# Stick-breaking heads with queries on partitions, reversed scans on VectorE, and four unread products ahead of each recurrence level

## The chip, the core and the metric

One NeuronCore of a Trainium2 chip runs the whole program in one launch. The metric is device time in microseconds (us), the median of several runs. The engines are TensorE (PE in the profile; PEld are its weight loads), VectorE (DVE), ScalarE (ACT), GpSimd (POOL) and SyncE (SP), which issues most DMAs. Each engine runs its own instructions in the order in which they are written, and waits at semaphores.

## What is computed

Two transformer blocks, one after the other, on 512 tokens of width 1024, each with a mixture of experts behind its mixer. The change lies in the mixer of the second block. It has eight stick-breaking heads (width 64) beside four heads of a gated recurrence (width 128); 16 meta tokens stand ahead of the 512. Cut to the stick-breaking heads:

```python
z = einsum('bhtd,bhsd->bhts', q, k) * scale
valid = (s_pos < t_pos) & (s_pos >= LEAD_PAD)
log_keep = where(valid, log_sigmoid(-z), 0.0)
log_tail = lax.cumsum(log_keep, axis=3, reverse=True) - log_keep
w = where(valid, exp(log_sigmoid(z) + log_tail), 0.0)
out = einsum('bhts,bhsd->bhtd', w, v)
```

With softplus(z) = log(1 + exp(-|z|)) + max(z, 0), the exponent of a weight is z minus the sum of the softplus over that key and all later ones. The recurrence is computed in seven levels per head: at each level the products of two decayed factors fill one more part of a 128x128 causal matrix of every 128-token tile.

## The kernel before

The second mixer is 10 turns (`TURNS`) of 4 places (`PLACES`), written out by hand on every engine. Turn i takes up stick-breaking head i, and each place of turns 1 to 7 holds one of the 28 recurrence levels, `step(n)`: GpSimd subtracts decays (`level_diff`), ScalarE exponentiates (`level_exp`), VectorE multiplies (`level_products`, which raises `level_ready`), TensorE takes four 128x128 products (bank L), and VectorE reads them one level later (`level_read`). At level 0 of a recurrence head TensorE also does KT and DG, at level 1 the output HO of the head before, at level 2 the state KV.

A stick-breaking head before: keys lie on partitions, queries along the columns, 1792 columns in five pieces. `scores` gives Z (TensorE), VectorE scales and masks it into `zw`, ScalarE takes Abs and Exp (`stick_exp`) and Ln (`stick_log`), VectorE adds max(z, 0) (`stick_logits`), GpSimd adds up the sums of later key blocks (`sums_of_blocks`), TensorE takes the sums over keys with a triangle of ones (`sums_behind`, bank R), VectorE subtracts them (`stick_subtract`), ScalarE exponentiates (`stick_weights`) and TensorE multiplies with the values (`stick_out`, bank SO). R of head i-1 and SO of head i-2 stand in turn i. Behind turn 7, in turns 8 and 9, come the last heads, the normed rows turned (`mixed_turned`, mT) and split into a high and a low part (`mixed_high` on ScalarE, `mixed_low` on VectorE), and then the output product (`out_product`), which needs mT 4 to 7 for its first half. The loading of the second block's expert weights waits for the last mT, which is issued 24 matmuls into that product. `unread_products(b, count)` issues products of constants whose result nobody reads; before, it is used in the routers and at the head of the expert stage.

```python
def step_after(i, place):
    return PLACES * (i - 1) + place if 1 <= i < SBH else None
```

## Time and profile before

| | us |
|---|---|
| median of 3 runs | 1741.87 (1740.36 to 1744.36) |
| the profiled execution's own time | 1742.63 |
| its span in the profile | 1740.9 |
| PE busy | 1607.4 (92%) |
| DVE busy | 819.9 (47%) |
| ACT busy | 335.7 (19%) |
| POOL busy | 238.3 (14%) |

Times in the profile count from the start of the span. The busy shares are means over stages that differ; the turns of the second mixer are the stretch from about 1029 to 1187 us, 9% of the span, and the rest of the page says little about them.

### The profile page before, as it was taken

What the parts mean: (1) busy time and instruction counts of PE and PEld (TensorE: products, weight loads), DVE (VectorE), ACT (ScalarE), POOL (GpSimd) and SP (SyncE); (2) the same over time, 40 slices, a digit from 0 to 9 for tenths busy, and PEclk for the clock granted to TensorE, in tenths of its full rate; (3) what the DMA queues carried; (4) which work ended last, traced back from release to release, by engine and by line L of the source; (5) the groups of instructions that cost most, each with busy time, mean ns of one, the idle gap of its engine ahead of it and who ended that gap; (6) DMA issues with size and microseconds to landing.
All of it is one profiled execution on the core that took longest, in us unless ns stands there. A gap on an engine that the chain in (4) does not pass through costs nothing.

```text
span 1740.9 us, 19130 instructions
## 1 busy us (share of the span) xinstructions
PE 1607.4 (92%) x7778; PEld 1030.6 (59%) x7778; DVE 819.9 (47%) x1360; ACT 335.7 (19%) x574; POOL 238.3 (14%) x298
## 2 busy tenths in 40 slices
PE   7999999999999896878599988999999998999996
PEld 5688888886888432333488875778643333333332
DVE  7898645536464511111743249985532322332233
ACT  3422000027100210100311154651201010000011
POOL 1100003200000310110200005781120000000000
PEclk9999999999999998999799999999999999999998
DMA  5122222220237999999422200015899999999993
GB/s 203 49 97 97 73 97 97 98 73 25 76 146 284 305 407 409 425 428 414 190 98 73 97 25 1 1 44 220 327 378 430 429 429 429 429 430 430 430 430 143
DMA packets 54080, 403.27 MB, mean 232 GB/s; under 512 B 13776, under 2 KB 15184, under 8 KB 25952
## 3 DMA queue, kind: packets, MB, share of 16 engines
q1 hardware_dynamic: 46560, 389.34, 55.6%
q0 software_dynamic: 7424, 12.61, 2.0%
q8 instruction: 66, 1.08, 0.2%
q14 instruction: 30, 0.25, 0.0%
HBM read 397.69 MB, written 16.81 MB: 238 GB/s over the span
## 4 chain that ended last, share of the span: by engine, by line
PE 72%; DMA 14%; DVE 5%; ACT 2%; issue 2%; POOL 2%; SPq 2%; POOLq 0%; DVEq 0%; ACTq 0%
PE bank L1751 38%; PE bank L738 13%; PE bank L753 6%; DMA arena<-in_expert_in 4%; PE bank L717 2%; DMA arena<-in_expert_gate 2%; DMA ring<-in_expert_up 2%; DMA arena<-in_expert_up 2%; DMA ring<-in_expert_gate 2%; DMA arena<-in_expert_out 2%; DMA ring<-in_expert_in 1%; PE bank L1743 1%; PE bank L718 1%; PE bank L920 1%; PE bank L1862 1%
## 5 line engine op out<-in xcount | busy, mean ns | idle before, releaser
L738 PE MATMUL bank<-arena 128*64 128x512 f32 x960 | 273.8, 613 | 30.1 <-DMA arena<-in_expert_in 12.3
L738 PE MATMUL bank<-ring,arena 128*64 128x512 f32 x576 | 184.1, 618 | 9.9 <-issue 5.4
L738 PEld LDWEIGHTS bank<-arena 128*64 128x64 f32 x960 | 84.0, 140 | 174.9 <-issue 173.9
L1127 DVE TENSOR_TENSOR resid<-resid,bank 128x512 f32<-128x512 f32 x120 | 80.7, 685 | 202.9 <-PE bank L718 202.9
L2435 DVE CAST ring_high<-ring 128x2048 fp32r<-128x2048 f32 x51 | 63.0, 1236 | 238.3 <-DMA ring<-in_stream_a 147.4
L2436 DVE TENSOR_TENSOR ring_low<-ring,ring_high 128x2048 fp32r<-128x2048 f32 x60 | 138.7, 2312 | 6.4 <-ACT ring_high L2107 4.5
L753 PE MATMUL bank<-arena 128*64 128x512 f32 x448 | 114.4, 595 | 14.3 <-DVE arena L1153 7.2
L1751 PE MATMUL bank<-ring_low,xn_high 128*128 128x512 f32 x288 | 113.1, 393 | 0.3 <-DVE ring_low L2436 0.3
L1751 PE MATMUL bank<-ring_high,xn_high 128*128 128x512 f32 x288 | 112.3, 390 | 0.0
L1751 PE MATMUL bank<-ring_high,xn_low 128*128 128x512 f32 x288 | 112.2, 390 | 0.0
L738 PEld LDWEIGHTS bank<-ring,arena 128*64 128x64 f32 x576 | 55.9, 141 | 70.6 <-issue 70.6
L1149 DVE TENSOR_TENSOR arena<-misc,bank 128x256 f32<-128x256 f32 (+1 forms) x32 | 17.6, 551 | 165.5 <-ACT misc L1033 142.5
L1235 POOL DMA_INDIRECT arena<-xn_rows,token_table x32 | 32.6, 1020 | 417.8 <-PE bank L920 382.4
L753 PE MATMUL bank<-ring,arena 128*64 128x512 f32 x288 | 78.6, 596 | 7.1 <-issue 4.5
L753 PEld LDWEIGHTS bank<-arena 128*64 128x64 f32 x448 | 39.4, 137 | 75.9 <-issue 73.0
L1751 PE MATMUL bank<-xn_low,ring_high 128*128 128x512 f32 x192 | 75.8, 395 | 2.3 <-DVE misc L2571 2.3
L1751 PE MATMUL bank<-xn_high,ring_low 128*128 128x512 f32 x192 | 75.5, 393 | 0.0
L1751 PE MATMUL bank<-xn_high,ring_high 128*128 128x512 f32 x192 | 75.4, 393 | 0.0
L1033 ACT ACTIVATE misc<-bank 128x256 f32<-128x256 f32 (+1 forms) x32 | 15.7, 490 | 295.2 <-PE bank L738 295.2
L1267 POOL TENSOR_SCALAR rstd<-ssq 128x1 f32<-128x1 f32 x25 | 11.7, 468 | 422.0 <-ACT arena L1366 259.0
L1119 DVE SCALAR_TENSOR_TENSOR y_low<-bank,gate_slot,y_high 128x512 fp32r<-128x512 f32 x32 | 24.0, 751 | 91.7 <-ACT y_high L1047 91.7
L717 PEld LDWEIGHTS bank<-y_high,spread 128*128 128x128 f32 x128 | 24.0, 187 | 71.7 <-issue 69.0
(395 smaller groups left out, 3067.2 us busy)
## 6 DMA issues: line engine op xcount, KB each, us to landing
ring<-in_stream_a SPq DMA_DIRECT2D x42, 1024.0 KB, 5.1
arena<-in_expert_gate SPq DMA_DIRECT2D x20, 2048.0 KB, 23.7
arena<-in_expert_in SPq DMA_DIRECT2D x18, 2048.0 KB, 27.6
arena<-in_expert_up SPq DMA_DIRECT2D x18, 2048.0 KB, 24.6
arena<-in_expert_down SPq DMA_DIRECT2D x18, 2048.0 KB, 25.1
ring<-in_expert_up SPq DMA_DIRECT2D x12, 2048.0 KB, 25.7
ring<-in_expert_down SPq DMA_DIRECT2D x12, 2048.0 KB, 25.4
ring<-in_expert_gate SPq DMA_DIRECT2D x12, 2048.0 KB, 25.3
```

Source lines behind the costliest of these rows:

```text
L717: nc.tensor.matmul(bank[bank_at][:, :], w, half_of(y_high[:, p % 2, :], half), start=first, stop=False)
L718: ins = nc.tensor.matmul(bank[bank_at][:, :], w, half_of(y_low[p % 2], half), start=False, stop=last)
L738: last = nc.tensor.matmul(h[side * SLOTS:(side + 1) * SLOTS, :], tokens[:, k, side * SLOTS:(side + 1) * SLOTS], w[:, k * 512:(k + 1) * 512 ...
L753: last = nc.tensor.matmul(bank[6 + n][side * SLOTS:(side + 1) * SLOTS, :], hidden[:, f, side * SLOTS:(side + 1) * SLOTS], w[:, f * D + n * ...
L920: last = nc.tensor.transpose(bank[k // 4][:, k % 4 * P:(k % 4 + 1) * P], m.xg[:, p % XG, k * P:(k + 1) * P], c("ident"))
L1119: V.scalar_tensor_tensor(half_of(y_low[p % 2], half), bank[6 + half][:, :], gate_slot[:, p:p + 1], half_of(y_high[:, p % 2, :], half).bitc ...
L1127: nc.vector.tensor_tensor(place, place, bank[bank_at][:, :], ALU.add).then_inc(m.moe_added, 1)
L1149: V.tensor_tensor(m.act[:, 0:m.width], m.sg[:, 0:m.width], up_of(m), ALU.mult).then_inc(m.act_ready, 1)
L1235: G.indirect_dma_start(m.xg[:, p % XG, :], None, m.xn_rows[:, :], bass.IndirectOffsetOnAxis(ap=m.token_table[:, p:p + 1], axis=0), bounds_ ...
L1751: ins = nc.tensor.matmul(b, left(k)[l_], right(k)[r_], start=(first and k == 0 and i == 0), stop=(last and k == KC // 2 - 1 and i == 2))
L2435: then(V.tensor_copy(hi, ring_raw[n % RING]))
L2436: V.tensor_tensor(lo, ring_raw[n % RING], hi.bitcast(F32), ALU.subtract).then_inc(weights_split, 1)
```

## The change

Queries now lie on partitions and keys along the columns, 1344 columns: four 128-column blocks of a query tile against its own keys, masked, and four "rest" pieces of 16, 144, 272 and 400 columns. So the sum over later keys runs along the columns. ScalarE scales the rest pieces from PSUM (`stick_scores`) and VectorE only the four masked blocks; ScalarE writes max(z, 0) as a Relu into `above_zero`; eight VectorE scans over reversed views (`stick_sums`) add both and run the sum, and one 1344-column subtraction gives the exponents. TensorE turns these in 14 transposes (`exponents_turned`, bank WT), ScalarE exponentiates what was turned, from PSUM into `w_turned` (`stick_weights`), and TensorE multiplies as before (`stick_out`). `sums_of_blocks`, `sums_behind`, `stick_logits` and `stick_subtract` are gone. The output of head i-1 now stands in turn i, one turn earlier, and there are 9 turns. Four unread 512-column products stand ahead of each level's wait for `level_ready`. The value projection takes 16 rows of the meta tile instead of 128. The last turned rows come in another order, and two of the last loads of projection weights wait for other units.

```diff
+REST_W = [META + t * P for t in range(NT)]
+REST_AT = [SEQ + sum(REST_W[:t]) for t in range(NT)]
+STICK = SEQ + sum(REST_W)
+SCORE_UNITS = ((), (0, 1, 2), (3,))
+TURNED = 10 * P + SEQ
+TURNED_UNITS = (((0, 0), (0, 1), (0, 2), (0, 3)), ((1, 1), (1, 2), (1, 3), (3, 3)), ((2, 2), (2, 3)))
+TURNED_AT = {at: SEQ * n + P * j for n, unit in enumerate(TURNED_UNITS) for j, at in enumerate(unit)}
...
-        zw = [at(arena, i * STICK, [STICK]) for i in range(3)]
+        zw = [at(arena, i * STICK, [STICK]) for i in (2, 3)]
+        above_zero = at(arena, STICK, [STICK])
+        w_turned = at(ring[1], 0, [TURNED])
...
-                    sp.wait_ge(psum_filled2, U2.filled(("R", SBH - 2, NT2 - 1)))
+                    sp.wait_ge(psum_filled2, U2.filled(("WT", SBH - 2, 3)))
+                if n == first + 2 * len(STREAM2) - 2:
+                    sp.wait_ge(psum_filled2, U2.filled(("SO", SBH - 1)))
...
+                def product(out, t, keys_):
+                    return nc.tensor.matmul(out, sbq[half, h // 2, t * P:(t + 1) * P], keys_, start=True, stop=True)
+                b = begin2(("Z", h, 0))
+                for t in range(NT):
+                    last_ = product(b[:, t * P:(t + 1) * P], t, sbk[half, h // 2, (t + 1) * P:(t + 2) * P])
+                end2(last_)
+                for j in (1, 2):
+                    b = begin2(("Z", h, j))
+                    for t in SCORE_UNITS[j]:
+                        a = REST_AT[t] - REST_AT[SCORE_UNITS[j][0]]
+                        last_ = product(b[:, a:a + REST_W[t]], t, sbk[half, h // 2, PAD:PAD + REST_W[t]])
                     end2(last_)
...
+            def exponents_turned(g, units):
+                pe.wait_ge(exponents_ready, g + 1)
+                e = zw[g % 2]
+                for j in units:
+                    b = begin2(("WT", g, j))
+                    if j < 3:
+                        for n, (s, t) in enumerate(TURNED_UNITS[j]):
+                            a = t * P if s == t else REST_AT[t] + META + s * P
+                            last_ = nc.tensor.transpose(b[:, n * P:(n + 1) * P], e[:, a:a + P], c("ident"))
+                    else:
+                        for t in range(NT):
+                            last_ = nc.tensor.transpose(b[0:META, t * P:(t + 1) * P], e[:, REST_AT[t]:REST_AT[t] + META],
+                                                        c("ident"))
+                    end2(last_)
             def stick_out(g):
-                pe.wait_ge(weight_ready, g + 1)
+                wait_read2(pe, ("WT", g, 3))
                 b = begin2(("SO", g))
                 for t in range(NT):
-                    for s in range(t + 2):
-                        a = STICK_AT[s] + (t - FIRST_T[s]) * P
-                        last_ = nc.tensor.matmul(b[:, t * SBD:(t + 1) * SBD], zw[g % 3][:, a:a + P],
-                                                 sbv[:, s, g * SBD:(g + 1) * SBD], start=(s == 0), stop=(s == t + 1))
+                    out_ = b[:, t * SBD:(t + 1) * SBD]
+                    for s in range(t + 1):
+                        a = TURNED_AT[s, t]
+                        nc.tensor.matmul(out_, w_turned[:, a:a + P], sbv[:, s + 1, g * SBD:(g + 1) * SBD],
+                                         start=(s == 0), stop=False)
+                    last_ = nc.tensor.matmul(out_, w_turned[0:META, META_AT + t * P:META_AT + (t + 1) * P],
+                                             sbv[0:META, 0, g * SBD:(g + 1) * SBD], start=False, stop=True)
                 end2(last_)
             def head_out(g):
...
+                b = begin2(("L", h, lv))
+                unread_products(b, 4)
                 pe.wait_ge(level_ready, n + 1)
-                b = begin2(("L", h, lv))
                 for t in range(NT):
...
                     if place == 0 and i < SBH:
                         scores(i)
-                    if sums_blocks(i, place):
-                        sums_behind(i - 1, sums_blocks(i, place))
-                    if place == 2 and i >= 2:
-                        stick_out(i - 2)
+                    if place == 3 and i >= 1:
+                        stick_out(i - 1)
                     if step_after(i, place) is not None:
                         step(step_after(i, place))
+                    if place in (1, 2) and i >= 1:
+                        exponents_turned(i - 1, (0, 1) if place == 1 else (2, 3))
                     if (i, place) == (SBH, 0):
                         for k in (4, 5):
                             mixed_turned(k)
                         head_out(HGH - 1)
+                        for k in (0, 1):
+                            mixed_turned(k)
                     if (i, place) == (SBH, 2):
-                        mixed_turned(6)
-            for k in TURN_ORDER[3:-1]:
-                mixed_turned(k)
-            out_product(0, (1, 0), lambda part: wait_read2(pe, ("mT", TURN_ORDER[4 * part + 3])),
-                        lambda: mixed_turned(TURN_ORDER[-1]))
+                        for k in (2, 6):
+                            mixed_turned(k)
+            mixed_turned(7)
+            out_product(0, (1, 0), lambda part: wait_read2(pe, ("mT", 3 if part else 7)), lambda: mixed_turned(3))
...
+            def stick_scores(h):
+                if h >= 2:
+                    act.wait_ge(psum_filled2, U2.filled(("WT", h - 2, 3)))
+                for j in (1, 2):
+                    b, ts = unit2(("Z", h, j)), SCORE_UNITS[j]
+                    a, end = REST_AT[ts[0]], REST_AT[ts[-1]] + REST_W[ts[-1]]
+                    read2(A.activation(zw[h % 2][:, a:end], b[:, 0:end - a], ACT.Copy, scale=SBD ** -0.5))
             def stick_exp(h):
                 v = sps[h % 2]
-                act.wait_ge(z_ready, h + 1)
-                A.activation(v, zw[h % 3], ACT.Abs).then_inc(act_step, 1)
+                wait_read2(act, ("Z", h, 0))
+                wait_read2(act, ("Z", h, 2))
+                A.activation(v, zw[h % 2], ACT.Abs).then_inc(act_step, 1)
                 act.wait_ge(act_step, 2 * h + 1)
                 A.activation(v, v, ACT.Exp, scale=-1.0).then_inc(act_step, 1)
             def stick_log(h):
                 v = sps[h % 2]
+                if h >= 1:
+                    act.wait_ge(sums_ready, h)
+                A.activation(above_zero, zw[h % 2], ACT.Relu).then_inc(log_ready, 1)
                 act.wait_ge(act_step, 2 * h + 2)
                 A.activation(v, v, ACT.Ln, bias=1.0).then_inc(log_ready, 1)
             def stick_weights(g):
-                wait_read2(act, ("R", g, NT2 - 1))
-                A.activation(zw[g % 3], zw[g % 3], ACT.Exp).then_inc(weight_ready, 1)
+                for j, unit in enumerate(TURNED_UNITS):
+                    b, w = unit2(("WT", g, j)), P * len(unit)
+                    read2(A.activation(w_turned[:, SEQ * j:SEQ * j + w], b[:, 0:w], ACT.Exp))
+                b = unit2(("WT", g, 3))
+                read2(A.activation(w_turned[0:META, META_AT:META_AT + SEQ], b[0:META, :], ACT.Exp))
...
-            def stick_subtract(g, blocks):
-                for s in blocks:
-                    b = unit2(("R", g, s))
-                    zs = zw[g % 3][:, STICK_AT[s]:STICK_AT[s] + STICK_W[s]]
-                    read2(V.tensor_tensor(zs, zs, b[:, 0:STICK_W[s]], ALU.subtract))
-            def stick_logits(h):
-                dve.wait_ge(log_ready, h + 1)
-                V.scalar_tensor_tensor(sps[h % 2], zw[h % 3], 0.0, sps[h % 2], ALU.max, ALU.add).then_inc(sp_ready, 1)
+                if h >= 2:
+                    dve.wait_ge(psum_filled2, U2.filled(("WT", h - 2, 3)))
+                b = unit2(("Z", h, 0))
+                read2(V.scalar_tensor_tensor(zw[h % 2][:, 0:SEQ].rearrange("p (t s) -> p t s", s=P),
+                                             b[:, :].rearrange("p (t s) -> p t s", s=P), SBD ** -0.5,
+                                             c("strict")[:, None, :].broadcast_to([P, NT, P]), ALU.mult, ALU.add))
+            def sums_from_last(v, a, w, initial):
+                part = v[:, a:a + w][:, ::-1]
+                return V.tensor_tensor_scan(part, part, above_zero[:, a:a + w][:, ::-1], initial, ALU.add, ALU.add)
+            def stick_sums(h):
+                v = sps[h % 2]
+                dve.wait_ge(log_ready, 2 * h + 2)
+                for t in range(NT):
+                    ins = sums_from_last(v, t * P, P, 0.0)
+                then(ins)
+                for t in range(NT):
+                    ins = sums_from_last(v, REST_AT[t], REST_W[t], v[:, t * P:t * P + 1])
+                ins.then_inc(sums_ready, 1)
+                dve.wait_ge(sums_ready, h + 1)
+                V.tensor_tensor(zw[h % 2], zw[h % 2], v, ALU.subtract).then_inc(exponents_ready, 1)
...
-                    if sums_blocks(i, place):
-                        stick_subtract(i - 1, sums_blocks(i, place))
-                    if place == 2 and 1 <= i < SBH or (i, place) == (1, 0):
-                        stick_logits(i if place else 0)
+                    if place == 2 and i < SBH:
+                        stick_sums(i)
+                    if place == 1 and i >= 2:
+                        head_sums(i - 2)
                     if (i, place) == (SBH, 1):
                         last_head_norm()
-                    if place == 1 and i >= 3:
-                        head_sums(i - 3)
+                        mixed_low(0)
+                        mixed_low(1)
                     if (i, place) == (SBH, 2):
+                        mixed_low(2)
                         mixed_low(6)
...
-            def sums_of_blocks(g):
-                v = sps[g % 2]
-                pool.wait_ge(sp_ready, g + 1)
-                for s in range(NT2 - 2, -1, -1):
-                    a, w, behind = STICK_AT[s], STICK_W[s], STICK_W[s + 1]
-                    ins = G.tensor_tensor(v[:, a + w - behind:a + w], v[:, a + w - behind:a + w], v[:, a + w:a + w + behind],
-                                          ALU.add)
-                    if s > 0:
-                        then(ins)
-                ins.then_inc(sums_ready, 1)
...
-                    if place == 3 and 2 <= i < SBH + 1:
+                    if place == 0 and i >= 2:
                         head_square(i - 2)
-                    if place == 2 and i >= 3:
-                        head_norm(i - 3)
-                    if place == 2 and 1 <= i < SBH or (i, place) == (1, 0):
-                        sums_of_blocks(i if place else 0)
+                    if place == 2 and i >= 2:
```

The three places of which the prediction speaks, as the instructions stand on their engines. First ScalarE in turn 5, from the rows of scores on. Before: the exponentials of the weights of head 3 (L2308), Abs and Exp of head 5 (L2297, L2299), the exponentials for recurrence head 3 (L2322 to L2329), a level's exponential (L2318) and Ln (L2304).

```order
L2308 ACTIVATE arena<-arena 128x1792
L2297 ACTIVATE misc<-arena 128x1792
L2299 ACTIVATE misc<-misc 128x1792
L2322 ACTIVATE chunk_decay<-arena 128x5
L2326 ACTIVATE ring<-arena 128x128 x4
L2329 ACTIVATE ring<-arena 128x512
L2318 ACTIVATE resid<-resid 128x512
L2304 ACTIVATE misc<-misc 128x1792
L2318 ACTIVATE resid<-resid 128x512
```

After: two copies of scores (L2320), Abs and Exp (L2326, L2328), the same recurrence exponentials (L2357 to L2364), level (L2353), Relu and Ln (L2334, L2336), level, and the exponentials of the weights of head 4 (L2341, the last of them L2343, not shown).

```order
L2320 ACTIVATE arena<-bank 128x432
L2320 ACTIVATE arena<-bank 128x400
L2326 ACTIVATE misc<-arena 128x1344
L2328 ACTIVATE misc<-misc 128x1344
L2357 ACTIVATE chunk_decay<-arena 128x5
L2361 ACTIVATE ring<-arena 128x128 x4
L2364 ACTIVATE ring<-arena 128x512
L2353 ACTIVATE resid<-resid 128x512
L2334 ACTIVATE arena<-arena 128x1344
L2336 ACTIVATE misc<-misc 128x1344
L2353 ACTIVATE resid<-resid 128x512
L2341 ACTIVATE ring<-bank 128x512 x2
```

The exponentials of the weights moved from ahead of Abs to behind Ln. Second TensorE at the end of turn 5. Before: a level (L2036), the second part of R (L1993, L1996), the next level, and the scores of head 6 (L1985).

```order
L2036 MATMUL bank<-resid 128x128 x4
L1993 MATMUL bank<-ring,cst 128x384
L1996 MATMUL bank<-ring,cst 128x256
L1993 MATMUL bank<-ring,cst 128x256
L1996 MATMUL bank<-ring,cst 128x128
L1993 MATMUL bank<-ring,cst 128x128
L2036 MATMUL bank<-resid 128x128 x4
L1985 MATMUL bank<-arena 128x512 x2
```

After: the last ten products of `stick_out` (L2022, L2024), the unread products (L1301), the level (L2055), and the scores of head 6 (L1987).

```order
L2022 MATMUL bank<-arena,ring 128x64 x3
L2024 MATMUL bank<-arena,ring 128x64
L2022 MATMUL bank<-arena,ring 128x64 x4
L2024 MATMUL bank<-arena,ring 128x64
L1301 MATMUL bank<-count_ones 128x512 x4
L2055 MATMUL bank<-resid 128x128 x4
L1987 MATMUL bank<-arena 128x128 x4
L1987 MATMUL bank<-arena 128x16
```

So `stick_out`, which waits for the exponentials of the weights, now stands ahead of the last level of a turn and of the next scores. Third VectorE in turn 0 and at the start of turn 1. Before: five scans for the decays, the keys (L2719, L2720), the two products that KT and HO need (`head_products`, L2813, L2815), the first level's products (L2769, L2774), and the scores of head 1.

```order
L2726 SCALAR_TENSOR_TENSOR arena<-cst,arena 128x128 x5
L2719 TENSOR_SCALAR arena<-arena,oml 128x528 x4
L2720 MEMSET arena 128x4x112
L2813 TENSOR_TENSOR ring<-ring,arena 128x512
L2815 TENSOR_TENSOR ring<-ring,arena 128x512
L2769 TENSOR_TENSOR resid<-resid,arena 128x4x64
L2774 TENSOR_TENSOR resid<-resid,arena 128x4x64
L2745 TENSOR_SCALAR arena<-bank,cst 128x512
```

After, from the keys' last instruction on: the eight scans and the subtraction of head 0 (L2784, L2796), then `head_products` (L2847, L2849) and the first level.

```order
L2757 MEMSET arena 128x4x112
L2784 SCALAR_TENSOR_TENSOR ring<-ring,arena 128x128 x4
L2784 SCALAR_TENSOR_TENSOR ring<-ring,arena 128x16
L2784 SCALAR_TENSOR_TENSOR ring<-ring,arena 128x144
L2784 SCALAR_TENSOR_TENSOR ring<-ring,arena 128x272
L2784 SCALAR_TENSOR_TENSOR ring<-ring,arena 128x400
L2796 TENSOR_TENSOR arena<-arena,ring 128x1344
L2847 TENSOR_TENSOR ring<-ring,arena 128x512
L2849 TENSOR_TENSOR ring<-ring,arena 128x512
L2803 TENSOR_TENSOR resid<-resid,arena 128x4x64
```

The sums of head 0 stand in front of the first level; they wait for that head's Ln.

## Rows read from the trace of the kernel before

**Rows 1.** The page, part 1: span and TensorE's share.

```profile
span 1740.9 us, 19130 instructions
```

**Rows 2.** Stretches: start, turn 2, turns 3 to 6, turn 7, tail.

```profile
core 0: us, PE busy (x) PEld busy (x) DVE busy (x) ACT busy (x) POOL busy (x), PEclk, DMA share, GB/s
1028.83:1060.36 31.53, 19.70 (x90) 13.88 (x88) 26.82 (x51) 21.40 (x29) 14.32 (x17) 0.78 0.00 1
1060.36:1080.75 20.39, 17.47 (x102) 13.18 (x101) 19.76 (x39) 9.51 (x10) 11.35 (x15) 1.00 0.00 1
1080.75:1154.54 73.79, 72.73 (x450) 57.65 (x449) 68.49 (x130) 41.81 (x53) 57.60 (x71) 1.00 0.00 1
1154.54:1169.80 15.26, 15.26 (x89) 11.68 (x90) 13.88 (x30) 8.42 (x8) 9.55 (x14) 1.00 0.00 1
1169.80:1187.19 17.39, 16.52 (x120) 14.01 (x119) 10.64 (x20) 8.36 (x12) 12.09 (x18) 1.00 0.65 242
```

**Rows 3.** The chain that ended last, turn 7: start, us, what.

```profile
1154.54 3.21 PE bank L1985 x10
...
1158.83 0.86 PE bank L1993 x2
...
1162.06 0.89 PE bank L2036 x8
1162.95 3.07 PE bank L2006 x28
```

**Rows 4.** Instructions in order of time, VectorE: start, us, instruction, idle before.

```profile
1101.18 0.74 DVE L2745 TENSOR_SCALAR arena<-bank,cst 128x512 f32<-128x512 f32 x1
...
1103.42 0.28 DVE L2747 SCALAR_TENSOR_TENSOR arena<-bank,cst 128x128 f32<-128x128 f32 x1
```

**Rows 5.** Groups by line and form in the turns: busy, mean ns, idle before.

```profile
L2758 DVE TENSOR_TENSOR arena<-arena,bank 128x512 f32<-128x512 f32 x16 | 10.6, 681 | 3.7 <-PE bank L1996 3.3 <-DVE resid L2792 0.2 <-DVE ring L2801 0.2
L2762 DVE SCALAR_TENSOR_TENSOR misc<-arena,misc 128x1792 f32<-128x1792 f32 x4 | 8.1, 2022 | 0.3 <-DVE ring L2801 0.2
```

**Rows 6.** In order of time, five scans of 128 columns alone, and beside GpSimd.

```profile
1032.03 1.69 DVE L2726 TENSOR_TENSOR_SCAN arena<-cst,arena 128x128 f32<-128x128 f32 x5
...
1047.05 3.63 DVE L2726 TENSOR_TENSOR_SCAN arena<-cst,arena 128x128 f32<-128x128 f32 x5
...
1044.79 3.87 POOL L2991 TENSOR_TENSOR ring<-ring 128x128 f32<-128x128 f32 x4 [3.41 <-DVE ring L2762]
```

**Rows 7.** A 4-column GpSimd operation beside VectorE's 1792 columns, and all twelve of it.

```profile
1111.89 2.38 DVE L2762 SCALAR_TENSOR_TENSOR ring<-arena,ring 128x1792 f32<-128x1792 f32 x1 [0.15 <-DVE resid L2792]
...
1112.47 1.85 POOL L2970 TENSOR_SCALAR rstd<-rstd 128x4 f32<-128x4 f32 x1
...
L2970 POOL TENSOR_SCALAR rstd<-rstd x12: 192/193/2047, 1094.3 to 1186.6; 128x4 f32<-128x4 f32 x12
```

**Rows 8.** In order of time, ScalarE in the start and in turn 6.

```profile
1036.76 1.26 ACT L2326 ACTIVATE ring<-arena 128x128 f32<-128x128 f32 x4
...
1139.62 0.63 ACT L2318 ACTIVATE resid<-resid 128x512 f32<-128x512 f32 x1 [7.81 <-POOL resid L3008]
...
1143.46 1.70 ACT L2299 ACTIVATE ring<-ring 128x1792 f32<-128x1792 f32 x1
1145.06 0.61 ACT L2318 ACTIVATE resid<-resid 128x512 f32<-128x512 f32 x1
```

**Rows 9.** In order of time, TensorE: unread products in the router.

```profile
1241.81 4.05 PE L1303 MATMUL bank<-count_ones 128*128 128x512 f16 x18
```

**Rows 10.** In order of time, TensorE in the start.

```profile
1038.87 1.12 PE L1911 MATMUL bank<-cst,ring 128*128 128x128 f32 x4 [5.13 <-DVE ring L2813]
...
1048.71 2.07 PE L1993 MATMUL bank<-ring,cst 128*128 128x512 f32 x2 [6.09 <-POOL ring L2991]
...
1052.09 1.02 PE L1993 MATMUL bank<-ring,cst 128*128 128x512 f32 x2
```

**Rows 11.** The chain that ended last, the tail.

```profile
1168.92 0.91 PE bank L2036 x8
...
1181.40 0.45 PE bank L1911 x4
1181.84 3.09 PE bank L2006 x28
...
1186.39 0.75 DVE state_low L2834
1187.19 5.74 PE bank L1751 x24
```

125 lines of the change are left out of this document (47 added, 78 removed).

## The prediction

> **What bounds the kernel now.** The span is 1740.9 us [rows 1]; the execution took 1742.63, the median of the runs is 1741.87. I read first the busy time by stretch [rows 2]: the turns run from 1028.83 to 1187.19. From turn 3 to 6 TensorE is busy 72.73 of 73.79 us and VectorE 68.49, so both are nearly full: 18.4 us a turn. In the start the granted clock is 0.78 of full and TensorE busy 19.7 of 31.5. Then I read the chain that ended last [rows 3, 11]: in turn 7 it stays on TensorE, and the tail is R, SO, the turned rows and one VectorE split ahead of the output product at 1187.19. What comes behind that product moves with it: the expert loads wait for the last mT, 24 matmuls into the product both before and after. So only the product's start counts.
>
> **What a head costs on each engine.** TensorE before: scores 3.21, SO 3.07; the first four of the nine R products (1920 columns) take 1162.06 - 1158.83 = 3.23, all 3072 columns 5.2; a level 0.89 [rows 3]. After: 3.21/1792 x 1344 = 2.4 for scores, 14 transposes at 0.45/4 [rows 11] = 1.6, SO 3.07 again (14 products, the narrow ones no cheaper). That is 11.5 against 7.1. The unread products take (4.05 - 0.38)/17 = 0.216 each [rows 9], the last one's length 0.38 taken off, so 0.86 a level and 3.5 a turn. TensorE gives back 1 us a turn net. Its sum by turn after: 7.1 + 4 x (0.89 + 0.86) + the recurrence's KT, DG, KV, HO (0.45, and 16 more 128-column products at 0.89 per four: 4.0 per seven levels, 2.3 a turn) = 16.4.
>
> VectorE before: scores 1101.18 to 1103.70 = 2.5 [rows 4], max and add 2.0, subtracting 1792 columns in five pieces about 2.5 (0.68 per 512) [rows 5]: 7.0. After: the masked block 0.7; scans: five of 128 columns in 1.69 [rows 6], 0.325 each from start to start; with 0.06 fixed that is 2.07 ns a column, so 1344 columns in eight scans are 2.8 + 0.5 = 3.3; the subtraction 1344/1792 x 2.02 = 1.5 [rows 5]; the link between the two sets of scans 0.15. Sum 5.7, of which 4.95 in one block. Reversed views are not in the trace; I take the forward price, bound it below by the same and above by double (3.3 more a head). GpSimd loses its 3.87 a head [rows 6].
>
> ScalarE: 1792 columns take 1.70, 512 take 0.61 [rows 8], so 0.85 ns a column; 1344 take 1.31. Abs, Exp, Relu, Ln are 5.2, the copies of scores 1.0, the weights' four exponentials 1.95. That is 8.2 against 6.8: ScalarE is far from full, but what matters is where they stand.
>
> **The loop that takes over.** From the order on ScalarE and TensorE: after Ln come a level's exponential (0.54) and the weights (1.95); `stick_out` waits for them (3.07 + 0.1), then unread (0.86), the level (0.89), scores of the next head (2.4 + 0.15 to the last end), last copy 0.5, Abs and Exp 2.65, a level 0.54, Relu and Ln 2.55. Sum 16.2 us a turn, in which no engine is full. The other branch, Ln to sums (4.95) to the level's products (0.67), ends 0.9 us before the unread products do. Into the loop fall, in walking the six turns: turn 2, `head_products` between sums and KT, +1.25; turn 3, the HO copy that ScalarE waits for (+1.1) and 2.0 of recurrence exponentials (1.26 for its four [rows 8], one of 512 and a short one); turn 4, HO on TensorE +1.8; turn 5, again 2.0; turn 6, KT's copy 0.57, KV 0.89 and WT waiting behind HO, +2.7; turn 7 none. Together 97.2 + 10.8 = 108 us. Before, turns 2 to 7 took 1169.80 - 1060.36 = 109.4 [rows 2]. Gain 1.4.
>
> **The start.** In turn 0 the sums of head 0 now stand ahead of `head_products`. ScalarE: copies from 1033.4 to 1034.4, Abs, Exp to 1037.1, recurrence exponentials to 1039.0, level 1039.5, Relu, Ln to 1042.1; sums to 1047.0; KT can start at 1047.7 where it started at 1038.87 [rows 10]. Before, the 9 us were mostly lost again: TensorE idled 6.09 us until 1048.71 for GpSimd's sums and then ran its first product at half speed (1.87 us for 0.86 of work, against the third pair) [rows 10]. After, level 0 ends near 1052.3 (the unread products run at half and then full speed), Ln of head 1 near 1055.9, its sums 1061.1, `stick_out` of head 0 at 1062.1, level 3 at 1063.9. Before, the scores of head 2 began at 1060.36. Loss 3.5.
>
> **The tail.** Before, 17.4 us from the last level to the product [rows 2, 11]: R and two SO (3.07 + 3.09), an exponential between. After: mT 4, 5, HO (waits for the last read; done 3.0 in), the copy and mT 0, 1 to 4.6, WT to 6.1, the weights on ScalarE to 7.4, SO to 10.6, the copy to 11.1; VectorE's squares and row sum to 12.5, then the split of mT 7 to 13.2. Gain 4.1. The load that now waits for the last SO and the re-reading of rows behind it have 11 us and more until they are used; without that cover they would cost about 5.
>
> **The value projection** still streams 512 columns a product: nothing.
>
> **Sharing between VectorE and GpSimd.** Rows 6 and 7 show it: five scans took 3.63 us instead of 1.69 beside GpSimd's sums, and a 4-column operation of GpSimd 1.85 instead of 0.193 beside 1792 columns of VectorE [rows 6, 7]. In the block of sums GpSimd has a level's two subtractions and a head's norm, about 3.1 us. Bounds: nothing, or 3.1 a turn. I take about 1.2; over the 0.9 of slack, and whole in turn 2, that is +1.8 in all.
>
> **Sum.** 3.5 - 1.4 - 4.1 + 1.8 = -0.2, against 1742.63; against the median 1741.7. I say 1741.5.
>
> **Rivals.**
> First, no change to speak of, as summed: 1738.4 to 1745.4, which is within 0.2% (3.5 us, about what a measurement of this kernel tells from no change). Chance 0.38.
> Second, faster: the 10.8 us that I put into the loop run beside it, and TensorE's own 16.4 a turn is the bound. 6 x 16.4 = 98.4 instead of 108, no toll from sharing: 1741.5 - 9.6 - 1.8 = 1730; half of it 1736. For it: GpSimd made ScalarE wait 7.81 us for a level in turn 6 [rows 8], and its sums are gone. Against: ScalarE's order is fixed, and so are `stick_out`'s wait and the three exponentials behind the scores. Chance 0.34.
> Third, slower: the block of sums meets GpSimd's work and is doubled as in rows 6: 3.3 becomes 7.1, less the slack 0.9, +2.9 a turn. Six turns are 17, less the 1.8 already in: 1757; half is 1749. It decides as soon as the block grows by over 0.9. Against: GpSimd has only 3.1 us there, where in that row it worked all the time. Chance 0.20.
> The Trainium skill ("SBUF — State Buffer", Who interferes with whom) says that the pair of ports which VectorE and GpSimd share is an exclusive lock held for the whole instruction, and that a VectorE instruction with two SBUF inputs contends with a GpSimd instruction that reads SBUF. By that rule each GpSimd instruction in the block adds its whole length, 3.1 less 0.9 a turn, 13 over six turns and 1753; rows 6 and 7 agree with it in kind.
> Fourth, reversed scans run at half the forward rate: +3.3 - 0.9 a turn, 1756. Chance 0.05.
> Fifth, in the walked turns TensorE waits about 2.8 us ahead of each `stick_out`; in the start a wait of 6.09 was followed by half speed [rows 10]. If the shorter ones are too, a turn's `stick_out`, unread products, level and half the scores would take up to 3 us more, 1758. Against: turn 2 had 2.9 us of TensorE idle at full clock [rows 2], and the unread products fill what is left. Chance 0.03.
>
> **How the numbers follow.** Faster by over 0.2%: the second case and 0.02 of the first's edge, 0.36. Slower: the third to fifth, 0.28, less 0.02 where the third adds under 3.5 us: 0.26. Same: 0.38. The likeliest alone is 1738.4 to 1745.4; the range, which leaves out the full second, third, fourth and fifth cases, is 1730 to 1753.
>
> **What the profile will show.** If right: ScalarE in a turn goes scores, Abs, Exp, level, Relu, Ln, level, weights without a gap, then idles while TensorE runs SO to scores; TensorE waits before L2022 for ScalarE's L2343; turns last 16 to 19 us; KT near 1047.7; the last level near 1171.7 and the output product near 1187, with a tail of 13 us. Scans of 128 columns 0.33 apart, POOL without its 0.5 to 1.3 us additions. Wrong: TensorE waiting for L2803 or L2796 (the third), its busy share at 98% in turns 3 to 6 (the second), scans at twice the length (the third or fourth), a clock under 1.00 in turns 2 to 7 (the fifth).

## The result and the profile after

The changed kernel takes **1778.42 us** (median of 4 runs, 1773.58 to 1780.31) beside 1743.11 us for the kernel before in the same session: ratio **1.0182**, 95% interval 1.0155 to 1.0208. It is slower by 35 us by the medians (the interval of the ratio says 27 to 36); forecast were 1741.5 and a range of 1730 to 1753. The profiled execution took 1779.51.

The page's first line, which answers to [rows 1]:

```profile
span 1777.8 us, 19350 instructions
```

The stretches of [rows 2] in the changed kernel (start, turn 2, turns 3 to 6, turn 7, tail), the columns as there:

```profile
1027.67:1067.68 40.01, 23.85 (x138) 19.06 (x137) 27.56 (x55) 25.82 (x41) 9.53 (x14) 0.70 0.00 1
1067.68:1089.38 21.70, 20.27 (x119) 16.41 (x119) 15.66 (x30) 10.65 (x16) 7.54 (x12) 0.84 0.00 1
1089.38:1187.38 98.00, 91.72 (x522) 73.98 (x521) 59.08 (x112) 47.35 (x77) 38.71 (x57) 0.81 0.00 1
1187.38:1207.70 20.32, 18.89 (x109) 15.06 (x109) 13.83 (x24) 9.01 (x13) 6.23 (x8) 0.83 0.16 53
1207.70:1221.97 14.27, 11.36 (x87) 9.70 (x85) 9.54 (x15) 7.10 (x13) 5.07 (x8) 0.97 0.06 14
```

Turns 2 to 7 last 21.70 + 98.00 + 20.32 = 140.0 us instead of 109.4, and PEclk, the third column from the end, stands at 0.81 to 0.84 where it was 1.00. Two halves of turns, cut where `stick_out` begins (from scores to there, and from there to the next scores), show where it falls:

```profile
1067.68:1078.70 11.02, 9.59 (x67) 7.36 (x67) 7.93 (x20) 8.71 (x13) 4.20 (x7) 1.00 0.00 1
1078.70:1089.38 10.68, 10.68 (x53) 9.04 (x53) 7.72 (x11) 1.94 (x4) 3.34 (x6) 0.68 0.01 2
...
1103.30:1113.19 9.89, 9.85 (x41) 7.95 (x41) 4.39 (x7) 1.21 (x3) 2.41 (x4) 0.59 0.01 2
```

In the first half TensorE idles 1.4 us and has the full clock. In the second it is busy without a gap, 10.68 of 10.68 us, and the clock is 0.68. TensorE in order of time, in the third of these stretches (start, us, instruction, idle before):

```profile
1103.34 0.43 PE L2022 MATMUL bank<-arena,ring 128*128 128x64 f32 x2 [1.70 <-ACT ring L2343]
1103.71 0.43 PE L2024 MATMUL bank<-arena,ring 16*128 16x64 f32 x2
1104.07 0.66 PE L2022 MATMUL bank<-arena,ring 128*128 128x64 f32 x4
1104.66 0.43 PE L2024 MATMUL bank<-arena,ring 16*128 16x64 f32 x2
1105.02 1.51 PE L2022 MATMUL bank<-arena,ring 128*128 128x64 f32 x6
...
1107.08 1.97 PE L2022 MATMUL bank<-arena,ring 128*128 128x64 f32 x8
1108.97 0.69 PE L2024 MATMUL bank<-arena,ring 16*128 16x64 f32 x2
1109.59 1.89 PE L1301 MATMUL bank<-count_ones 128*128 128x512 f16 x4
1111.28 1.91 PE L2055 MATMUL bank<-resid 128*128 128x128 f32 x8
1113.12 5.22 PE L1987 MATMUL bank<-arena 64*128 64x128 f32 x16
```

Two things are to be seen. A pair of instructions on the meta tokens (L2024, 16 rows: `16*128`; the 14 f32 products are 28 instructions) takes 0.36 us from its start to the next one's (1103.71 to 1104.07) at full clock; the same pair on 128 rows takes 0.22, as the run with full rows will show, and the instructions behind it take some 0.14 less in all (eight of them 0.89 instead of 1.03). And some 2 us after the wait of 1.70 the clock falls to 1.2 GHz, for the rest of `stick_out`, the unread products, the level and all scores: from start to start 1.69, 1.84 and 5.15 us for what takes 0.86, 0.89 and 2.7 at 2.4 GHz. (A row's own length runs past the next start, so rows of one kind are compared by their starts, or with rows of the same kind.) This is the worst of the six turns. In the others too the clock falls inside `stick_out`, behind waits of 0.68 to 1.71 us, but the scores behind it run at full clock or nearly so.

The end of the chain in the tail, which answers to [rows 11] (start, us, what):

```profile
1215.51 0.43 PE bank L2022 x2
...
1219.46 0.36 PE bank L2024 x2
1219.82 0.60 PE bank L1913 x4
...
1221.97 8.56 PE bank L1753 x24
```

The last `stick_out` runs here at full clock and still takes 1219.82 - 1215.51 = 4.31 us. The output product begins at 1221.97 instead of 1187.19, and its first 24 matmuls take 8.56 us instead of 5.74.

### The profile page after: what moved, and what is told of

The parts are those of the page before. It is cut to its first block, busy times and chain, and to the rows that moved or that the text cites. A ratio compares the mean times of both kernels' runs of the same rounds, so it can differ in the third digit from the quotient of the medians.

```text
span 1777.8 us, 19350 instructions
## 1 busy us (share of the span) xinstructions
PE 1635.1 (92%) x7906; PEld 1053.3 (59%) x7906; DVE 804.4 (45%) x1328; ACT 345.4 (19%) x622; POOL 197.3 (11%) x266
## 4 chain that ended last, share of the span: by engine, by line
PE 75%; DMA 13%; ACT 4%; DVE 3%; issue 2%; SPq 2%; POOL 1%; POOLq 0%; DVEq 0%; ACTq 0%
PE bank L1753 38%; PE bank L736 14%; PE bank L751 6%; DMA ring<-in_expert_in 3%; PE bank L715 2%; DMA arena<-in_expert_in 2%; DMA arena<-in_expert_gate 2%; DMA ring<-in_expert_up 2%; DMA arena<-in_expert_up 2%; PE bank L2022 2%; DMA ring<-in_expert_gate 2%; PE bank L1301 1%; PE bank L918 1%; PE bank L1745 1%; PE bank L1987 1%
## 5 line engine op out<-in xcount | busy, mean ns | idle before, releaser
L736 PE MATMUL bank<-arena 128*64 128x512 f32 x960 | 272.7, 610 | 28.2 <-DMA ring<-in_expert_in 10.9
L715 PE MATMUL bank<-y_high,spread 128*128 128x512 f32 x128 | 62.3, 487 | 0.0
## 6 DMA issues: line engine op xcount, KB each, us to landing
ring<-in_expert_up SPq DMA_DIRECT2D x12, 2048.0 KB, 25.5
```

The lines of the kernel that those rows point to most:

```text
L715: nc.tensor.matmul(bank[bank_at][:, :], w, half_of(y_high[:, p % 2, :], half), start=first, stop=False)
L736: last = nc.tensor.matmul(h[side * SLOTS:(side + 1) * SLOTS, :], tokens[:, k, side * SLOTS:(side + 1) * SLOTS], w[:, k * 512:(k + 1) * 512 ...
```

## The experiments

Each kernel is compared with the kernel before on the same chip. That kernel itself differed by up to 5.7 us from chip to chip, so "over", the difference of the two medians, is the column to compare kernels by. A ratio and its interval come from all runs of a session, so a ratio is not exactly the quotient of the two medians. "Five turns" is the time from the scores of head 2 to those of head 7, and the clock is the granted one over that stretch.

| kernel | median, us | over, us | ratio (95%) | five turns, us | clock |
|---|---|---|---|---|---|
| before | 1743.11, 1739.28, 1744.97, 1744.52 (four sessions) | 0 | 1 | 94.10 | 1.00 |
| the change | 1778.42 | 35.3 | 1.0182 (1.0155 to 1.0208) | 119.70 | 0.81 |
| change, no unread products | 1767.18 | 27.9 | 1.0161 (1.0110 to 1.0211) | 115.36 | 0.74 |
| before, with unread products | 1751.95 | 12.7 | 1.0066 (1.0034 to 1.0099) | 104.95 | 1.00 |
| change, ten ahead of `stick_out` | 1765.10 | 25.8 | 1.0149 (1.0119 to 1.0178) | 106.93 | 0.97 |
| change, no meta products | 1746.22 | 6.9 | 1.0052 (1.0024 to 1.0081) | 99.22 | 0.93 |
| change, full rows | 1755.85 | 10.9 | 1.0056 (1.0036 to 1.0076) | 104.49 | 0.92 |
| ten ahead of `stick_out` only | 1763.83 | 18.9 | 1.0108 (1.0088 to 1.0128) | 107.01 | 0.86 |
| `stick_out` behind scores | 1808.84 | 63.9 | 1.0362 (1.0340 to 1.0384) | 142.13 | 0.72 |
| the same, no unread products | 1804.79 | 59.8 | 1.0345 (1.0324 to 1.0365) | 135.43 | 0.68 |
| before, with narrow rows | 1762.61 | 18.1 | 1.0111 (1.0084 to 1.0138) | 106.49 | 0.89 |
| padded, no unread products | 1754.77 | 10.3 | 1.0071 (1.0045 to 1.0098) | 105.90 | 0.77 |
| padded, ten ahead of `stick_out` | 1749.99 | 5.5 | 1.0036 (1.0020 to 1.0051) | 97.43 | 0.95 |
| padded, ten and the unread ones | 1752.44 | 7.9 | 1.0044 (1.0022 to 1.0065) | 99.44 | 1.00 |

**The unread products apart.** First the change without them, then the kernel before with them.

```diff
-                unread_products(b, 4)
```

> The changed kernel without the four unread products ahead of each recurrence level. Theory A (TensorE's clock falls to its lower level in and behind stick_out because TensorE waited just ahead of it): the unread products fill the other waits, so without them the granted clock of turns 2 to 7 is no better than now and the kernel is about as slow or slower, 1778 to 1800 us. Theory B (the rows of ScalarE and TensorE make one loop per turn and the unread products stand on it, at half clock 1.8 us each): turns shorten by 0.9 to 1.8 us, 1765 to 1772. If the clock rises to 1.00 without them, both fall and the products themselves are at fault.

```diff
+                b = begin2(("L", h, lv))
+                unread_products(b, 4)
                 pe.wait_ge(level_ready, n + 1)
-                b = begin2(("L", h, lv))
```

> The kernel before with the same four unread products ahead of each of the 28 recurrence levels, and nothing else. TensorE was busy 72.73 of 73.79 us in turns 3 to 6, so the products cannot hide: 28 x 0.86 = 24 us if TensorE paces every turn, so 1760 to 1768; if waits for VectorE take them up, 1745 to 1755. Clock 1.00 in turns 2 to 7 either way. It tells how much of the 35 us belongs to the products alone.

Put into the kernel before they cost 12 us (TensorE there is busy without a gap at 1.00). Taken out of the change they bring its excess from 35.3 to 27.9, but the intervals of the two ratios overlap, so this is not clear of noise; in the traces the five turns are 4.3 us shorter, 0.9 a turn, as theory B said. The clock is no higher with them gone (0.74 against 0.81), so they hold some of it. The later pairs say the same (0.86 without them against 0.97 with them, and 0.95 against 1.00), and in none of them is the kernel clearly faster with them.

**`stick_out`: the wait or the narrow products.** Ten unread products ahead of its wait, then the change without the four 16-row products per head (the output lacks the meta tokens' values in the stick heads).

```diff
+                b = begin2(("SO", g))
+                unread_products(b, 10)
                 wait_read2(pe, ("WT", g, 3))
-                b = begin2(("SO", g))
```

> The changed kernel with ten more unread products (2.2 us at full clock) in stick_out ahead of its wait for ScalarE's exponentials, so that TensorE is not idle there. Theory A (the wait ahead of stick_out brings the clock down): clock near 1.00 in the stretch from stick_out to the next scores, which takes about 7.5 instead of 10 us, 15 to 20 us less in all: 1758 to 1765. Theory C (the narrow 64-column products of stick_out, with 16-row ones between, bring it down by themselves): the clock still falls in stick_out and the time stays within 5 us of the changed kernel, 1773 to 1785.

```diff
-                        nc.tensor.matmul(out_, w_turned[:, a:a + P], sbv[:, s + 1, g * SBD:(g + 1) * SBD],
-                                         start=(s == 0), stop=False)
-                    last_ = nc.tensor.matmul(out_, w_turned[0:META, META_AT + t * P:META_AT + (t + 1) * P],
-                                             sbv[0:META, 0, g * SBD:(g + 1) * SBD], start=False, stop=True)
+                        last_ = nc.tensor.matmul(out_, w_turned[:, a:a + P], sbv[:, s + 1, g * SBD:(g + 1) * SBD],
+                                                 start=(s == 0), stop=(s == t))
```

> The changed kernel leaves out the four 16-row products of each head with the meta tokens' values, so that its output lacks them. They take 0.36 us a pair at full clock where the others take 0.22, 1.4 us a head with what they leave behind. Theory C (the narrow products bring the clock down): stick_out keeps full clock or loses it later, and 8 x (1.4 + up to 2) = 11 to 27 us are saved: 1750 to 1767. Theory A: the clock falls as before, only the products' own time goes, 8 to 11 us: 1767 to 1771.

Both brought most of the clock back. The first came out at the upper edge of theory A's range, the second below theory C's. The second is the largest gain of any single edit: the excess goes from 35.3 to 6.9 us (23 us by the ratios). At full clock `stick_out` takes 2.28 us in it where the change's takes 4.24 (start to start, in TensorE's order of time), so 16 us of the gain are the length of the products and what they leave behind, in eight heads, and 7 to 12 the clock. TensorE in it, in order of time:

```profile
1097.06 3.29 PE L2022 MATMUL bank<-arena,ring 128*128 128x64 f32 x20 [1.70 <-ACT ring L2341]
1100.14 1.89 PE L1301 MATMUL bank<-count_ones 128*128 128x512 f16 x4
1101.85 1.07 PE L2053 MATMUL bank<-resid 128*128 128x128 f32 x8
```

The same wait of 1.70, and the clock falls again (1.89 for the unread products), but the level behind them is back at full clock (1.07). So neither the wait nor the narrow products alone explained the change.

**16 rows, or four products more.** The four are kept at full length, on 128 rows (the output's meta part is wrong).

```diff
-                    last_ = nc.tensor.matmul(out_, w_turned[0:META, META_AT + t * P:META_AT + (t + 1) * P],
-                                             sbv[0:META, 0, g * SBD:(g + 1) * SBD], start=False, stop=True)
+                    last_ = nc.tensor.matmul(out_, w_turned[:, TURNED_AT[0, t]:TURNED_AT[0, t] + P],
+                                             sbv[:, 1, g * SBD:(g + 1) * SBD], start=False, stop=True)
```

> The four products of 16 rows in each stick_out are replaced by four of 128 rows (the tile of keys 0 a second time), so the meta tokens' part of the output is wrong and the number of products, 14, stays. Theory N (the narrow rows: 16 of 128 rows of the array keep TensorE from holding its clock): stick_out at full clock takes about 14 x 0.22 = 3.1 us, the clock by 20 us stays above 0.90 in most of turns 2 to 7, and the time comes near that of the kernel without these products, 1750 plus 6 x 0.9 = 1755. Theory M (four more products behind a wait, whatever their rows): no change, 1775 to 1780, clock 0.6 to 0.9 from 1060 on. Theory W (the wait ahead decides alone): no change either.

It came to 1755.85 as theory N said, 22 to 24 us faster than the change (by the ratios, by the excess) with as many products; some 9 of it are their length in eight heads. It also bears on what the wait does. Turn 4, with a wait of 0.68 us, and then turn 3, with one of 1.70:

```profile
1115.95 0.43 PE L2022 MATMUL bank<-arena,ring 128*128 128x64 f32 x2 [0.68 <-ACT ring L2343]
...
1118.01 1.06 PE L2022 MATMUL bank<-arena,ring 128*128 128x64 f32 x8
1118.90 0.39 PE L2024 MATMUL bank<-arena,ring 128*128 128x64 f32 x2
1119.12 1.03 PE L1301 MATMUL bank<-count_ones 128*128 128x512 f16 x4
...
1094.75 0.43 PE L2022 MATMUL bank<-arena,ring 128*128 128x64 f32 x2 [1.70 <-ACT ring L2343]
...
1097.04 1.91 PE L2022 MATMUL bank<-arena,ring 128*128 128x64 f32 x8
```

Behind this short wait `stick_out` stays at 2.4 GHz throughout; behind the long one its last products run at half of that. The other turns agree in the main and not without exception: behind the wait of 0.68 us in turn 6 the clock falls too (the last eight and two instructions take 1.10 and 0.43 instead of 0.89 and 0.22), and behind the one of 1.45 in turn 2 it does not. In the change itself, with its narrow rows, it fell behind waits of 0.68 as well.

**Narrow rows in the kernel before.** The opposite test: nothing of the change, only the products of the padded first block of keys cut to 16 rows (the output leaves out the meta tokens' values). No wait stands there, and the number of instructions is the same.

```diff
-                        last_ = nc.tensor.matmul(b[:, t * SBD:(t + 1) * SBD], zw[g % 3][:, a:a + P],
-                                                 sbv[:, s, g * SBD:(g + 1) * SBD], start=(s == 0), stop=(s == t + 1))
+                        rows = slice(0, P if s else META)
+                        last_ = nc.tensor.matmul(b[:, t * SBD:(t + 1) * SBD], zw[g % 3][rows, a:a + P],
+                                                 sbv[rows, s, g * SBD:(g + 1) * SBD], start=(s == 0), stop=(s == t + 1))
```

> The kernel before, with the four products per head on the padded first block of keys cut from 128 rows to 16 (the output leaves the meta tokens' values out of the stick heads). No wait stands ahead of its stick_out, and sums of 128 rows stand on both sides. Theory N (narrow rows alone lower TensorE's clock): clock under 0.95 in turns 2 to 7 and 1760 or more. Rival NW (narrow rows cost length always, and the clock only where a wait or other narrow work stands ahead): the clock stays 1.00, stick_out takes 4.1 to 4.3 instead of 3.07, and as TensorE is full the eight of them add about 8 to 10: 1750 to 1753. Rival 0: a product of 16 rows costs no more than one of 128: 1742.

It costs 18.1 us. TensorE in order of time, one head whose `stick_out` ran at full clock and one in which it fell:

```profile
1089.56 4.31 PE L2007 MATMUL bank<-arena 16*128 16x64 f32 x28
1093.71 1.11 PE L2037 MATMUL bank<-resid 128*128 128x128 f32 x8
...
1129.64 5.09 PE L2007 MATMUL bank<-arena 16*128 16x64 f32 x28
1134.53 2.02 PE L2037 MATMUL bank<-resid 128*128 128x128 f32 x8
1136.34 1.49 PE L1993 MATMUL bank<-ring,cst 128*128 128x384 f32 x2
```

At full clock the 28 instructions take 4.15 from start to start (1089.56 to 1093.71) where [rows 3] had 3.07: 1.08 a head, 8.6 for eight. The other 9.5 are the clock, which falls here with no wait ahead of `stick_out` at all (TensorE waits 0.6 us in the whole stretch from 1058 to 1180). Theory N held, and the rival that said "length only, 1750 to 1753" fell.

**The fill without the unread products.**

> No unread products ahead of the levels, ten ahead of stick_out's wait. Theory W (the 1 to 3 us of waiting ahead of stick_out is what costs the clock, and the products ahead of levels only cost time): the clock is as in the run with ten such products and the levels' products kept (0.91 to 1.00), and the 24 levels of turns 2 to 7 give back 0.4 us each on the loop: 1765 less 10 = 1755. Rival U (the levels' products do their part of holding the clock): the clock by 20 us falls under 0.85 and the time is 1765 or more.

1763.83, which looks like a time between the two theories, but on this chip the kernel before was 5.7 us slower than on the one that 1765 came from. By the excess it is 18.9 us. Dropping the levels' products took 7.4 off the change's 35.3 and covering the wait 9.5, which leaves 18.4: in time the two add up. The clock is another matter: it goes from 0.97 to 0.86, and in three of six stretches of 20 us from 1060 on it is under 0.85, as rival U said.

**Breaking the loop.** `stick_out` of head h moves behind the scores of head h+2, its copy and the norm's steps after it, with and without the unread products.

```diff
+def out_at(i, place):
+    if place == 0 and i >= 2:
+        return i - 2
+    return SBH - 1 if (i, place) == (SBH, 3) else None
...
-                    if place == 3 and i >= 1:
-                        stick_out(i - 1)
+                    if out_at(i, place) is not None:
+                        stick_out(out_at(i, place))
```

> stick_out of head h moves from the end of turn h+1 to behind the scores of head h+2 (the last one stays), its copy behind that head's Abs and Exp, the norm's three steps one place later; nothing else changes. Theory L (a loop of ScalarE, stick_out, scores sets the turn, and the wait in front of stick_out costs the clock): the weights are long ready when stick_out comes, it no longer waits, clock above 0.9 and turns of 18 us or less where they are 23.3: 1778 less 25 to 35 = 1743 to 1753. Rival N (the narrow products lower the clock wherever they stand): still 0.7 to 0.8 in the stretch behind them, turns above 20 us, 1765 or more.

> The same move of stick_out, and no unread products ahead of the levels. Theory L: the loop is now VectorE's sums to a level's products to the next sums; without the unread products a level costs 0.89 on TensorE, the turn is 16.5 to 17.5 us and the time 1735 to 1745, the first version under before's. Rival U (the levels' products hold the clock): the clock falls below 0.85 in most 20 us from 1060 on and the time is above that of the version with them.

The theory of a loop to be broken fell: +64 and +60 us against the kernel before. Of rival U in the second run only the clock came out (0.68); the time was 4 us less than with the unread products, not more. TensorE in order of time, with the move alone:

```profile
1123.16 5.22 PE L1993 MATMUL bank<-arena 64*128 64x128 f32 x16
1128.31 0.69 PE L2028 MATMUL bank<-arena,ring 128*128 128x64 f32 x2
...
1133.29 1.97 PE L2028 MATMUL bank<-arena,ring 128*128 128x64 f32 x8
```

VectorE right after, with the idle time before the instruction:

```profile
1125.96 0.42 DVE L2811 TENSOR_TENSOR resid<-resid,arena 128x256 f32<-128x256 f32 x1
1139.43 0.73 DVE L2834 COPY_PREDICATED resid<-cst,bank 128x512 f32<-128x512 uint32 x1 [13.06 <-PE bank L2061]
```

and the waits of TensorE from 1064 to 1230 us in that kernel (us in total, times, longest):

```profile
PE bank L2061 <- DVE resid L2816: 11.0, 5, 4.3
PE bank L2061 <- DVE resid L2811: 5.0, 1, 5.0
PE bank L1919 <- DVE ring L2855: 4.5, 1, 4.5
```

`stick_out` no longer waits, yet here and in two more of the six turns scores (64 rows) and `stick_out` (64 columns) run at half clock from start to end, in the others `stick_out` falls in its second half. As both now stand ahead of a level, VectorE waits 13.06 us for it; then its block of sums stands ahead of the next level's products and TensorE waits for those, 20.5 us in these rows. The place at the end of a turn was the better one.

**Zero-padded meta rows.** The exponentials and values of the meta tile are padded with zeros to 128 rows, which computes the reference, and the three ways to place unread products are run with it.

```diff
+                if t == 0:
+                    A.activation(sbv[:, 0, :].rearrange("p (t s) -> p t s", s=P),
+                                 c("ident")[:, None, :].broadcast_to([P, NT, P]), ACT.Copy, scale=0.0).then_inc(zeroed, 1)
+                    act.wait_ge(zeroed, 1)
...
+                if g == 0:
+                    A.activation(w_turned[:, META_AT:META_AT + SEQ].rearrange("p (t s) -> p t s", s=P),
+                                 c("ident")[:, None, :].broadcast_to([P, NT, P]), ACT.Copy, scale=0.0).then_inc(zeroed, 1)
+                    act.wait_ge(zeroed, 2)
...
-                    last_ = nc.tensor.matmul(out_, w_turned[0:META, META_AT + t * P:META_AT + (t + 1) * P],
-                                             sbv[0:META, 0, g * SBD:(g + 1) * SBD], start=False, stop=True)
+                    last_ = nc.tensor.matmul(out_, w_turned[:, META_AT + t * P:META_AT + (t + 1) * P],
+                                             sbv[:, 0, g * SBD:(g + 1) * SBD], start=False, stop=True)
```

> The changed kernel with the meta tokens' products padded to 128 rows by zeros, which computes the reference, and no unread products ahead of the levels. From the run with full rows (1755.85) and the 11 us that leaving the unread products out gave: 1745 if both effects add. Rival C (with the wait of 1.7 ahead of stick_out uncovered and no unread products, the clock falls again): 1752 or more, and windows of 20 us under 0.90.

> The same, and ten unread products ahead of stick_out's wait, so that TensorE has work there. Theory W (full rows and a covered wait keep the clock whole): clock 1.00 in all 20 us from 1060 to 1180, stick_out 3.1 us in each turn, 1738 to 1744. Rival D (VectorE's block of sums and the loop over ScalarE set the turn, whatever the clock): as without the ten products, within 3 us of that run.

> The same as the last, with the four unread products ahead of each level kept as in the change. If they only lengthen the loop (24 levels of turns 2 to 7, about half of them on the path, 0.86 each): 8 to 12 us above the last one. Rival U (they keep the clock where it would fall): equal or below it.

The last is the run that matters most: full clock from turn 2 to the end of the tail. Its start, its turns 2 to 7, and its tail:

```profile
1027.41:1065.21 37.80, 22.31 (x153) 18.13 (x153) 27.31 (x55) 27.20 (x44) 8.36 (x12) 0.77 0.00 1
1065.21:1182.30 117.09, 112.94 (x808) 90.42 (x808) 90.33 (x167) 67.28 (x106) 54.84 (x79) 1.00 0.03 10
1182.30:1197.29 14.99, 12.09 (x97) 10.10 (x95) 9.46 (x15) 7.11 (x13) 4.96 (x8) 1.00 0.07 15
```

27 us of the 35 are gone, at the price of 2.16 us of extra products a turn. Without unread products at the levels the clock is 0.95 and the time 2.5 us less, within the intervals the same, and not the 8 to 12 that were expected; that run itself missed its 1738 to 1744 and its clock of 1.00. Without any unread products the clock is 0.77 and the time 1754.77, as rival C said: full rows alone do not keep the clock. No version came under the kernel before: the best is slower by 0.36% (0.20 to 0.51).

## Why the prediction was wrong

**The step that failed** is the assumption of full clock in turns 2 to 7. It was considered as the fifth rival, with the right engine, place and signature, and given a chance of 0.03 and a price of 3 us a turn at most; it cost about 4 (below), behind waits that were shorter than forecast (0.68 to 1.71 us, not 2.8). The reasons given against it were turn 2 of the kernel before, which kept its clock beside 2.9 us of idle time [rows 2], and the unread products. The first was a stretch full of wide products (that this kept its clock is my reading, no run shows it apart); what the change puts behind its waits is 14 products of 64 columns, four of them on 16 rows, then scores on 64 rows. The second was wrong: in turn 3 the unread products of a level ran at half speed themselves (a row of 1.89 us, and 1.03 at full clock).

**Its size.** The mean clock of turns 2 to 7 is (21.70 x 0.84 + 98.00 x 0.81 + 20.32 x 0.83) / 140.0 = 0.818. A share of 0.364 of the 140.0 us was therefore at half clock, 51 us, in which half the time, 25.5, was lost if TensorE was the bound there; it was busy almost without a gap in those halves of the turns. For the narrow rows 1.1 a turn goes off (`stick_out` in the tail takes 4.24 from start to start, with full rows 3.17), six times 6.6: 140.0 - 25.5 - 6.6 = 107.9. Forecast were 108 for the loop and 1.8 for sharing, 109.8. The padded kernel at full clock gives another estimate. Its turns 2 to 7 take 117.1 us, and the ten products ahead of `stick_out` end behind the last exponential there; in turn 6 (ScalarE, then TensorE, in order of time):

```profile
1156.88 0.59 ACT L2352 ACTIVATE ring<-bank 16x512 f32<-16x512 f32 x1
...
1158.84 0.33 PE L2023 MATMUL bank<-arena,ring 128*128 128x64 f32 x2
```

That is 1.37 us, and in the six turns 0.34 to 1.37, together 4.6, which leaves 112.5. The two estimates lie on either side of 109.8. So the loop's length was right within some 3 us, and the clock and the narrow rows are nearly the whole of the miss of 30 us in the turns.

**"SO 3.07 again (14 products, the narrow ones no cheaper)"** was a term mis-sized: 4.31 in the chain for the same number of instructions (from start to start 4.24, and 3.17 with full rows). The narrow ones are dearer, not just no cheaper. The Trainium skill ("TensorE: Matmul & The Clock Gate", Why this matters for your kernels) gives a single product of 32 rows the time of one of 128; no trace here shows one alone, and in a row of mixed ones the runs say 0.36 a pair against 0.22.

**The start.** KT begins at 1046.54 (forecast 1047.7). The scores of head 2 begin at 1067.68 instead of 1063.9, since the clock fell in the first `stick_out` too: it took 5.7 us, and the products and the level behind it 3.5 instead of 1.75. In the padded kernel they begin at 1065.21 with the fill.

**The tail** was forecast at 13.3 and took 14.27; the narrow rows of its `stick_out` (1.1) account for it, and in the full-rows kernel the tail takes 13.3. Not forecast were the 2.8 us that the output product's first 24 matmuls lose at the lower clock (granted over its first 10 us: 0.70); with full rows and full clock in the tail 1.6 of them stay (7.35 instead of 5.74). The balance is then 34.8 (the product's start, 1221.97 - 1187.19) + 2.8 = 37.6 against 1779.51 - 1742.63 = 36.9 measured.

**VectorE and the port** (the third rival): TensorE waited for ScalarE's weights 7.6 us in turns 2 to 7, six times and at the place foretold, and for VectorE once, 0.6. The eight scans, alone at the start, take 1.38 + 2.29 = 3.67 where 3.3 was forecast and the double would be 6.6 (the fourth rival fell), and the subtraction 1.56 for 1.5. In turns 2 to 7 the eight scans took 3.85 to 4.35 us, and 5.38 in the last, where GpSimd worked beside them. So the block did grow, in turns 4 and 7 by more than the slack of 0.9, as the third rival feared. Groups of the changed kernel in turns 2 to 7 (busy, mean ns, idle before); the two VectorE rows are those of three of the six heads:

```profile
L2022 PE MATMUL bank<-arena,ring 128*128 128x64 f32 x120 | 23.8, 345 | 7.6 <-ACT ring L2343 7.6
...
L2796 DVE TENSOR_TENSOR arena<-arena,ring 128x1344 f32<-128x1344 f32 x3 | 4.7, 1557 | 0.1
L2784 DVE TENSOR_TENSOR_SCAN ring<-ring,arena 128x128 f32<-128x128 f32 x12 | 4.5, 434 | 1.0 <-ACT ring L2336 0.9 <-DVE resid L2826 0.2
```

Sharing is visible in single places, as in the full-rows kernel, where `head_products`' second operation took 1.77 beside GpSimd instead of 0.68, but it did not set the time: TensorE's one wait for VectorE is 0.6. **TensorE's pace** (the second rival) would have needed 16.4 us a turn; the shortest of any changed kernel (with padded rows) was 17.76.

**The value projection** and the loads moved behind later units cost nothing that the trace shows.

**What stays open.** Ten more products, padded rows and full clock still leave the change 8 us above the kernel before. Against the trace of the kernel before, the scores of head 2 begin 4.9 us later, turns 2 to 7 are 7.7 longer, the tail is 2.4 shorter, and the output product's first 24 matmuls take 1.6 more. At most 4.6 of it is the fill; no kernel was run that has the clock without fill. Whether the 64 columns of `stick_out` or the 64 rows of scores count more for the clock was not told apart, nor whether it is the few rows themselves that lower it or the 0.14 us by which each such pair is longer.

## What to carry to other kernels

A term of the sum that reads "the same products as before" has to be held against rows and columns, not only against their number: cutting a padded product to its true 16 rows cost 18 us in a kernel that was otherwise left alone. Where a change puts narrow products behind a wait, price the clock for everything that stands behind them until wide work comes, and treat it as likely, not as a remainder. Of the unread products, those ahead of the wait in front of `stick_out` gained most here (9.5 us in the change by the medians, 4.8 in the padded kernel); those ahead of every level cost 12 us in the kernel before and nowhere made a kernel clearly faster.

## What the runs showed of the hardware

TensorE's clock fell in stretches in which it was busy without a gap (10.68 of 10.68 us at 0.68, and in the kernel before with narrow rows, with no wait ahead). In the turns it had by then done `stick_out`'s products of 64 columns, mostly with some on 16 rows, or scores on 64 rows; with full rows and no unread products it fell too (0.77). Behind a long wait it was low as well: 15.49 us ahead of KT in the start, and then 1.71 us for eight instructions that take 0.89. And a pair of instructions on 16 rows between pairs on 128 takes 0.36 us instead of 0.22, so in this kernel padding to full rows with zeros is faster as well as safer for the clock.
